# HGRN2 sample states: forget-gate multiply on GpSimd during the first four attention levels, instead of on VectorE in the loop behind them

## The chip, the cores and the metric

The kernel runs on one core of a Trainium2 chip, with its five engines: TensorE (PE in the rows, PEld for its weight loads), VectorE (DVE), ScalarE (ACT), GpSimd (POOL) and SyncE (SP). The metric is the device time of one launch in microseconds, lower is better.

## The reference, cut to what matters

The program is one inference step of a two-layer decoder trunk, for 256 prompt positions and 8 sample rows of one token each. Each layer has three mixer branches (RWKV-7, HGRN2, spatial gating), a merge, and a PEER expert block. The change is in HGRN2. Its state update per sample row, one token long, is this line with a single position:

```python
b = jnp.cumsum(l_c, axis=1)                       # l_c = log of the forget gate
...
b_last = b[:, -1]
s = (jnp.exp(b_last)[..., None] * s
     + jnp.einsum("bshk,bshv->bhkv", k_c * jnp.exp(b_last[:, None] - b), v_c))
```

For a sample row this is S = f * S + k v^T, with four heads of a 128 by 128 state, float32 throughout. The product f * S is the forget-gate multiply that the change moves. For the prompt the same recurrence is computed in chunks of 128 positions; its attention matrix, with a decay between every pair of positions, is built in seven "levels" of block halving.

## The kernel before

The kernel is written engine by engine, in a fixed order, with semaphores between the engines; nothing is scheduled by a planner. `S["name"]` is a semaphore. On VectorE, `done(ins, name, n)` lets the instruction raise the semaphore and then waits for it, `step(ins)` does the same with a semaphore of its own, and a bare `tt(...)` (tensor_tensor, printed as L1291) goes on without a wait.

**The levels.** For each of seven levels VectorE runs two subtractions of cumulated log gates (`lev_in`), ScalarE takes their exponential (`lev_exp`), VectorE multiplies by keys and by queries (two instructions, `lev_x`), and TensorE forms the product, 16 matmul records into banks 0 and 1 (`att_mm`), with a piece of a gate projection behind it. VectorE masks each bank into T5 or VS (`att_evac`), and GpSimd adds that to AT_ (L1818, `at_add`), two additions of 128x512 per level. T5 and VS are reused by the next level, so the masking of level n waits for the addition of level n-1. In VectorE's order a level therefore reads: mask, mask, multiply, multiply, subtract, subtract, where the subtractions belong to the level behind. The names M1, M2 are used below for the two multiplications, S1, S2 for the two subtractions, A0, A1 for GpSimd's two additions.

**The sample states.** `shs(b)` is the state of sample row b, 128 x 512 floats. ScalarE's queue loads the eight from HBM (L1101, L1102, semaphore `shs_in`) ahead of the levels. EB holds the exponentials of the cumulated log gates; for the sample columns that is the forget gate itself (`eb_done`). Behind the levels, and behind the two chunks of the prompt's output, TensorE broadcasts the value row of sample b over 128 partitions into bank 4 or 5 (an 8x512 matmul, two records, `vb_mm`), the broadcast of b waiting for `vb_evac` of b-2. VectorE then runs three instructions per b: shs = shs * f (not waited for), T5 = bank * k, shs = shs + T5. When all eight are done TensorE multiplies the states by the queries, 64 matmul records with one moving column (`hso_mm`), and from there the work goes on to a norm, to the spatial gating and to the branch merge.

GpSimd runs besides this the low halves of split weights (L1810) early in the layer and of the experts' weights (L1822) late in it.

Of the kernel before, what the change touches and what calls it, by code (L numbers as in the profile page):

```python
# [21 lines left out]
ALU = mybir.AluOpType  # L22
# [3 lines left out]
P = 128  # L26
D_MODEL = 1024
KD = D_MODEL // P
SEQ, DEC, DEPTH = 256, 8, 2
# [77 lines left out]
def build(nc, d):  # L107
    ctx = ExitStack()
    with ctx:
# [47 lines left out]
        def at(off, *dims):  # L157
            n = 1
            for x in dims:
                n *= x  # L160
            assert off + n <= ARENA, (off, n)
            v = arena[:, off:off + n]
            if len(dims) == 2:
                v = v.rearrange("p (a b) -> p a b", a=dims[0])
            if len(dims) == 3:
                v = v.rearrange("p (a b c) -> p a b c", a=dims[0], b=dims[1])
            return v
# [57 lines left out]
        HV = {n: at(o + i * NW * T, NW, T) for i, n in enumerate(names)}  # L225
# [8 lines left out]
        def shs(b):  # L234
            return SHA[:, b] if b < 5 else SHB[:, b - 5]
# [35 lines left out]
        def tka(*dims):  # L271
# [23 lines left out]

        names = """par_in smalls_in lb_in lb_exp mix_sq mix_ss mix_std h_ready shift_out z_mm z_evac xv_mm
            xv_evac zs_ready lora_in lora_mm lora_evac decay_in decay_out kk_sq kk_ss kk_std prep_done bon_done
            bon_mm mat_mm mat_evac l_mm l_evac p_mm p_evac ml_ready xt_mm xt_add x_mm x_add late_gates w_hi w_low w_plow x_done tok_mm tok_evac y_mm y_evac u_mm
            u_evac o_evac s_mm s_evac sq_mm sq_evac rq_in sr_in sr_done sr_out so_out so_in ot_mm gn_m gn_sq gn_v
            gn_std yr_done hg_in hg_sig f_ready f_ln b_ready eb_done lev_in lev_exp lev_x att_mm att_evac kh_in  # L300
            kh_exp kh_done ht_mm ht_evac ho_evac hs_mm hs_evac shs_in vs_mm vs_evac vb_mm vb_evac hso_mm hso_evac
# [5 lines left out]
        S = {n: ctx.enter_context(nc.semaphore(n)) for n in dict.fromkeys(names)}  # L307
# [23 lines left out]
        def over(ap, n):  # L331

            return ap.rearrange("p (a b) -> p a b", b=1).broadcast_to([ap.shape[0], ap.shape[1], n])
# [15 lines left out]
        def ring_pair(p):  # L349

            return p % RINGP if p < 37 else (p - 37) % RINGP
# [921 lines left out]
        def _(dve):  # L1273
# [5 lines left out]
            def step(ins):  # L1279

                steps[0] += 1
                ins.then_inc(S["dve_step"], 1)
                dve.wait_ge(S["dve_step"], steps[0])

            def done(ins, name, n):

                ins.then_inc(S[name], 1)
                dve.wait_ge(S[name], n)

            def tt(out, a, b, op):  # L1290
                return dve.tensor_tensor(out, a, b, op)  # L1291
# [40 lines left out]
            for l in range(DEPTH):  # L1332
# [174 lines left out]
                FF, U1, U2, BC, EB, KH, QH = (HV[n] for n in ("FF", "U1", "U2", "BC", "EB", "KH", "QH"))  # L1507
# [49 lines left out]
                for lev in range(1, LEV_H + 1):  # L1557
                    hx = HV[f"HX{lev % 2}"]
                    b = 1 << (lev - 1)
# [21 lines left out]
                dve.wait_ge(S["at_add"], 2 * LEV_H * (l + 1))  # L1581
                for b in range(DEC):
                    dve.wait_ge(S["vb_mm"], l * DEC + b + 1)
                    tt(shs(b), shs(b), over(EB[:, :, SEQ + b], P), ALU.mult)
                    step(tt(T5, bank[4 + b % 2][:, :].rearrange("p (a b) -> p a b", a=NW),
                            over(HG[:, 4:8, SEQ + b], P), ALU.mult))
                    done(tt(shs(b), shs(b), T5, ALU.add), "vb_evac", l * DEC + b + 1)
# [214 lines left out]
        @block.gpsimd  # L1802
        def _(pool):

            for l in range(DEPTH):

                for c in range(RT, 25):
                    pool.wait_ge(S["w_hi"], l * NSPLIT + c + 1)
                    at_tile = 2 * ring_pair(c // 2) + c % 2
                    pool.tensor_tensor(ring_r[:, at_tile], ring[:, at_tile], WZ[c % 3].bitcast(F32), ALU.subtract)\  # L1810
                        .then_inc(S["w_plow"], 1)

                for lev in range(1, LEV_H + 1):
                    for c in range(NHC):
                        pool.wait_ge(S["att_evac"], l * 2 * (LEV_H + 1) + 2 * lev + c + 1)
                        if lev > 1:
                            pool.wait_ge(S["at_add"], l * 2 * LEV_H + 2 * (lev - 2) + c + 1)
                        pool.tensor_tensor(AT_[:, c], AT_[:, c], (T5, VS)[c], ALU.add).then_inc(S["at_add"], 1)  # L1818

                def low(u, b, slot, turn):  # L1820
                    pool.wait_ge(S["hi_done"], turn + (l * NU + u + 1))
                    pool.tensor_tensor(WHL[:, b, 1], raw[:, slot], WHL[:, b, 0].bitcast(F32), ALU.subtract)\  # L1822
                        .then_inc(S["plo_done"], 1)

                with pool.Fori(0, GU // SLOTS) as i:
                    for b in range(SLOTS):
                        low(b, b % 2, b, i * SLOTS)
                with pool.Fori(0, NODD // 2) as i:
                    for b in (1, 3):
                        low(GU + b, 1, b, i * SLOTS)  # L1830
# [97 lines left out]
```

## Time and profile before

| what | value |
|---|---|
| runs shown | 3088.27, 3092.19, 3093.40 us |
| their median | 3092.19 us |
| the profiled execution's own time | 3089.66 us |
| its span, first to last instruction | 3087.8 us |
| busy share PE / DVE / ACT / POOL | 92% / 61% / 37% / 20% |
| mean granted TensorE clock | 0.952 |

The busy shares are averages over the whole span. The change concerns two short stretches in each of the two layers: the levels, from about 378 to 416 us, and the loop over the sample states, from about 435 to 453 us, with the same again about 1529 us later. A row of a timeline has its start, the duration in us, the engine, the line, the operation, out<-in with shapes, a count of instructions run together as one row, and in brackets the idle time ahead of it and what ended that. The granted clock is TensorE's, as a share of 2.4 GHz; 0.50 is 1.2 GHz.

### The profile page before, as it was taken

The page shows a single profiled execution, that of the slowest core. Times are in us where ns is not written, and L with a number is a line of the kernel's source. Part 1 is how long each engine was busy: PE and PEld are TensorE (multiplying, and loading weights), DVE is VectorE, ACT ScalarE, POOL GpSimd, SP SyncE. Part 2 cuts the span into 40 slices and gives each one's busy share as a digit, 9 for nine tenths or more (in the row PEclk, how much of TensorE's full clock was granted, in tenths as well). Part 3 has the DMA queues.
Part 4 walks back from the last instruction along what each step waited for, and adds up shares of the span by engine and source line. Part 5 has one row for each costly group of instructions (what it writes and reads, how often), then busy time and mean ns, then how long its engine had stood idle before and what let it go on. Part 6 is the DMA issues. An engine that isn't in the chain of part 4 may idle for free.

```text
span 3087.8 us, 55843 instructions
## 1 busy us (share of the span) xinstructions
PE 2842.2 (92%) x21498; PEld 2659.4 (86%) x21498; DVE 1878.0 (61%) x2841; ACT 1145.9 (37%) x1822; POOL 602.9 (20%) x242
## 2 busy tenths in 40 slices
PE   7699778899999999999987996798999999999998
PEld 6688557799899999999986885577999999999997
DVE  4854664259856666666658537443696666666665
ACT  3312211045543335555443112101455433455553
POOL 0400020018842220000021001100388322200000
PEclk9899887999999999999998998789999999999998
DMA  5222212335543335555551222114355433455553
GB/s 198 82 85 69 88 42 82 123 117 163 159 141 122 122 121 172 182 178 179 160 201 45 95 69 86 58 55 150 123 160 161 135 119 120 129 177 181 179 179 120
DMA packets 114369, 396.02 MB, mean 128 GB/s; under 512 B 18194, under 2 KB 19730, under 8 KB 112852
## 3 DMA queue, kind: packets, MB, share of 16 engines
q1 hardware_dynamic: 105444, 381.28, 37.9%
q10 hardware_dynamic: 8816, 13.27, 1.4%
q8 instruction: 70, 1.15, 0.1%
q14 instruction: 39, 0.32, 0.0%
HBM read 385.44 MB, written 8.53 MB: 128 GB/s over the span
## 4 chain that ended last, share of the span: by engine, by line
PE 61%; issue 22%; POOL 10%; DVE 6%; ACT 1%; DMA 0%; POOLq 0%; ACTq 0%; SPq 0%; DVEq 0%
PE bank L450 61%; POOL WHL L1822 8%; DVE arena L1291 4%; POOL ring_r L1810 1%; ACT arena L954 1%; POOL arena L1818 1%; DVE arena L1516 0%; DVE arena L1400 0%; DVE arena L1295 0%; DVE hT L1299 0%; DVE arena L1299 0%; DVE NRM L1309 0%; DVE arena L1532 0%; DMA COM<-com 0%; DVE arena L1365 0%
## 5 line engine op out<-in xcount | busy, mean ns | idle before, releaser
L450 PE MATMUL bank<-HHL,WHL 128*128 128x264 f32 x6144 | 795.6, 287 | 27.2 <-POOL WHL L1822 21.5
L450 PEld LDWEIGHTS bank<-HHL,WHL 128*128 128x128 f32 x6144 | 763.7, 190 | 37.5 <-POOL WHL L1822 28.6
L450 PE MATMUL bank<-AHL,WHL 128*128 128x264 f32 x6144 | 748.7, 284 | 0.0
L450 PEld LDWEIGHTS bank<-AHL,WHL 128*128 128x128 f32 x6144 | 748.5, 188 | 0.0
L1822 POOL TENSOR_TENSOR WHL<-raw,WHL 128x1024 fp32r<-128x1024 f32 x188 | 484.8, 2586 | 997.6 <-ACT WHL L954 997.6
L954 ACT ACTIVATE WHL<-raw 128x1024 fp32r<-128x1024 f32 x512 | 542.3, 1060 | 336.1 <-PE bank L450 334.4
L1291 DVE TENSOR_TENSOR WHL<-raw,WHL 128x1024 fp32r<-128x1024 f32 x324 | 394.8, 1218 | 26.2 <-ACT WHL L954 26.2
L450 PEld LDWEIGHTS bank<-arena 64*64 64x64 f32 (+3 forms) x3200 | 274.8, 165 | 136.7 <-DVE arena L1291 99.4
L450 PE MATMUL bank<-arena 64*64 64x64 f32 (+7 forms) x3200 | 301.3, 256 | 96.2 <-DVE arena L1291 91.2
L954 ACT ACTIVATE arena<-bank 128x264 f32<-128x264 f32 (+6 forms) x248 | 110.5, 463 | 728.8 <-PE bank L450 636.7
L1291 DVE TENSOR_TENSOR AHL<-ACTS,AHL 128x528 fp32r<-128x528 f32 x256 | 181.3, 708 | 277.9 <-ACT AHL L954 277.9
L954 ACT ACTIVATE ACTS<-bank 128x264 f32 (+32 forms) x438 | 147.9, 338 | 489.8 <-PE bank L450 489.5
L450 PE MATMUL bank<-hT,ring 128*128 128x264 f32 (+1 forms) x1280 | 315.7, 399 | 14.2 <-DVE hT L1299 11.7
L1291 DVE TENSOR_TENSOR arena<-arena 128x512 f32<-128x512 f32 (+9 forms) x254 | 263.1, 1055 | 105.5 <-ACT arena L954 59.5
L450 PEld LDWEIGHTS bank<-hT,ring 128*128 128x128 f32 x1280 | 242.4, 194 | 62.3 <-DVE hT L1299 12.5
L450 PE MATMUL bank<-OHG,OHE 128*128 128x128 bf16 x1584 | 209.0, 297 | 0.0
L1291 DVE TENSOR_TENSOR ACTS<-ACTS,bank 128x240 f32<-128x240 f32 (+21 forms) x132 | 71.2, 539 | 184.0 <-ACT ACTS L954 183.8
L450 PEld LDWEIGHTS bank<-OHG,OHE 128*128 128x128 bf16 x1584 | 168.7, 118 | 8.0
L954 ACT ACTIVATE AHL<-ACTS 128x528 fp32r (+1 forms) x256 | 160.9, 628 | 2.1 <-PE bank L450 2.1
L450 PE MATMUL bank<-arena,ring 128*128 128x264 f32 x640 | 151.2, 397 | 7.8 <-DVE arena L1291 4.4
L1291 DVE TENSOR_TENSOR arena<-bank,arena 128x264 f32<-128x264 f32 (+2 forms) x132 | 74.7, 578 | 128.2 <-PE bank L450 127.5
L450 PEld LDWEIGHTS bank<-arena,ring 128*128 128x128 f32 x640 | 125.3, 196 | 31.2 <-DVE arena L1291 4.6
(128 smaller groups left out, 2104.9 us busy)
## 6 DMA issues: line engine op xcount, KB each, us to landing
raw<-down SPq DMA_DIRECT2D x256, 512.0 KB, 3.5
raw<-up SPq DMA_DIRECT2D x256, 512.0 KB, 3.5
ring<-wm SPq DMA_DIRECT2D x100, 1024.0 KB, 5.0
arena<-hs ACTq DMA_DIRECT2D x2, 1280.0 KB, 5.8
o_hs<-arena ACTq DMA_DIRECT2D x2, 1280.0 KB, 4.5
arena<-cm SPq DMA_DIRECT2D x2, 1160.0 KB
arena<-rs SPq DMA_DIRECT2D x4, 512.0 KB, 6.2
o_rs<-arena ACTq DMA_DIRECT2D x4, 512.0 KB, 5.6
```

What stands on the lines that cost most here:

```text
L450: return pe.matmul(out, lhsT, rhs, start=start, stop=stop)
L954: return act.activation(out, in_, fn, **kw)
L1291: return dve.tensor_tensor(out, a, b, op)
L1810: pool.tensor_tensor(ring_r[:, at_tile], ring[:, at_tile], WZ[c % 3].bitcast(F32), ALU.subtract)\
L1818: pool.tensor_tensor(AT_[:, c], AT_[:, c], (T5, VS)[c], ALU.add).then_inc(S["at_add"], 1)
L1822: pool.tensor_tensor(WHL[:, b, 1], raw[:, slot], WHL[:, b, 0].bitcast(F32), ALU.subtract)\
```

## The change

VectorE's loop loses the multiply by the forget gate, and waits for the new semaphore `shs_f` in its place. GpSimd gets the eight multiplies, two behind its two additions in each of levels 1 to 4. Ahead of the first it waits for the loaded states and for EB. Nothing else is changed; no transfer is added or moved.

```diff
@@ VectorE, the loop behind the levels
                 for b in range(DEC):
                     dve.wait_ge(S["vb_mm"], l * DEC + b + 1)
-                    tt(shs(b), shs(b), over(EB[:, :, SEQ + b], P), ALU.mult)
+                    dve.wait_ge(S["shs_f"], l * DEC + b + 1)
                     step(tt(T5, bank[4 + b % 2][:, :].rearrange("p (a b) -> p a b", a=NW),
                             over(HG[:, 4:8, SEQ + b], P), ALU.mult))
                     done(tt(shs(b), shs(b), T5, ALU.add), "vb_evac", l * DEC + b + 1)
@@ GpSimd, at the end of each level's two additions
                         pool.tensor_tensor(AT_[:, c], AT_[:, c], (T5, VS)[c], ALU.add).then_inc(S["at_add"], 1)
+                    if lev <= 4:
+                        if lev == 1:
+                            pool.wait_ge(S["shs_in"], 32 * (l + 1))
+                            pool.wait_ge(S["eb_done"], l + 1)
+                        for b in (2 * lev - 2, 2 * lev - 1):
+                            pool.tensor_tensor(shs(b), shs(b), over(HV["EB"][:, :, SEQ + b], P), ALU.mult)\
+                                .then_inc(S["shs_f"], 1)
```

On GpSimd, in the levels of the first layer, a single run of 14 additions stands before:

```order
15 L1818 TENSOR_TENSOR arena<-arena 128x512 x14
16 L1825 UNCONDITIONAL_BRANCH
```

and after the change:

```order
15 L1818 TENSOR_TENSOR arena<-arena 128x512 x2
16 L1824 TENSOR_TENSOR arena<-arena 128x512 x2
17 L1818 TENSOR_TENSOR arena<-arena 128x512 x2
18 L1824 TENSOR_TENSOR arena<-arena 128x512 x2
19 L1818 TENSOR_TENSOR arena<-arena 128x512 x2
20 L1824 TENSOR_TENSOR arena<-arena 128x512 x2
21 L1818 TENSOR_TENSOR arena<-arena 128x512 x2
22 L1824 TENSOR_TENSOR arena<-arena 128x512 x2
23 L1818 TENSOR_TENSOR arena<-arena 128x512 x6
24 L1832 UNCONDITIONAL_BRANCH
```

The additions (L1818) of levels 1 to 4 now each have two gate multiplies (L1824) behind them; those of levels 5 to 7 stand in one run as before.

On VectorE, in the loop over the sample states of the first layer, the difference between the two kernels is this (arena<-arena is the gate multiply and the addition, arena<-bank,arena the product with k):

```order
 L1291 TENSOR_TENSOR arena<-arena,bank 128x512
-L1291 TENSOR_TENSOR arena<-arena 128x512
 L1291 TENSOR_TENSOR arena<-bank,arena 128x512
-L1291 TENSOR_TENSOR arena<-arena 128x512 x2
+L1291 TENSOR_TENSOR arena<-arena 128x512
 L1291 TENSOR_TENSOR arena<-bank,arena 128x512
-L1291 TENSOR_TENSOR arena<-arena 128x512 x2
+L1291 TENSOR_TENSOR arena<-arena 128x512
```

One of three instructions is gone for each state; the product with k is now the first one behind TensorE's broadcast.

## Rows read from the trace of the kernel before

**Rows 1.** Timeline of VectorE in the levels: start, us, engine, line, operation

```profile
378.26 2.50 DVE L1291 TENSOR_TENSOR arena<-arena 128x512 f32<-128x512 f32 x4
380.95 0.69 DVE L1291 TENSOR_TENSOR arena<-bank,arena 128x512 f32<-128x512 f32 x1 [0.19 <-PE bank L450]
...
382.63 3.77 DVE L1291 TENSOR_TENSOR arena<-arena 128x512 f32<-128x512 f32 x4
...
387.41 0.69 DVE L1291 TENSOR_TENSOR arena<-bank,arena 128x512 f32<-128x512 f32 x1 [0.26 <-PE bank L450]
388.13 3.79 DVE L1291 TENSOR_TENSOR arena<-arena 128x512 f32<-128x512 f32 x4
```

**Rows 2.** Timelines of VectorE and GpSimd in one level, in short windows

```profile
381.72 1.27 POOL L1818 TENSOR_TENSOR arena<-arena 128x512 f32<-128x512 f32 x1 [263.90 <-DVE arena L1291]
...
382.95 1.71 POOL L1818 TENSOR_TENSOR arena<-arena 128x512 f32<-128x512 f32 x1
...
382.63 0.90 DVE L1291 TENSOR_TENSOR arena<-arena 128x512 f32<-128x512 f32 x1
...
383.46 1.75 DVE L1291 TENSOR_TENSOR arena<-arena 128x512 f32<-128x512 f32 x1
```

**Rows 3.** Timeline of GpSimd and VectorE early in the first layer

```profile
111.03 1.26 DVE L1291 TENSOR_TENSOR arena<-V,arena 128x1056 f32<-128x1056 f32 x1
...
112.32 3.30 DVE L1291 TENSOR_TENSOR arena<-arena 128x1056 f32<-128x1056 f32 x1
...
112.16 2.34 POOL L1810 TENSOR_TENSOR ring_r<-ring,WZB 128x1024 fp32r<-128x1024 f32 x1 [8.18 <-ACT WZB L954]
```

**Rows 4.** Timeline of GpSimd in the levels, one level of the steady ones

```profile
387.23 2.94 POOL L1818 TENSOR_TENSOR arena<-arena 128x512 f32<-128x512 f32 x2 [2.57 <-DVE arena L1291]
```

**Rows 5.** Timeline of TensorE in the levels: a middle level and the last

```profile
385.26 2.05 PE L450 MATMUL bank<-arena 128*128 128x128 f32 x16 [1.68 <-DVE arena L1291]
...
412.81 3.58 PE L450 MATMUL bank<-arena 128*128 128x128 f32 x16 [3.46 <-DVE arena L1291]
```

**Rows 6.** Line 1102, the later of the two loads of the states

```profile
L1102 ACTq DMA_DIRECT2D arena<-hs x2: 450/450/450, 363.5 to 1892.7; - x2
...
DMA to landing us min/median/max: 7.2/7.3/7.4
```

**Rows 7.** Timeline of VectorE in the loop over the sample states

```profile
436.37 0.69 DVE L1291 TENSOR_TENSOR arena<-arena 128x512 f32<-128x512 f32 x1 [3.23 <-PE bank L450]
436.98 0.68 DVE L1291 TENSOR_TENSOR arena<-bank,arena 128x512 f32<-128x512 f32 x1
437.69 1.42 DVE L1291 TENSOR_TENSOR arena<-arena 128x512 f32<-128x512 f32 x2
...
442.67 0.69 DVE L1291 TENSOR_TENSOR arena<-arena 128x512 f32<-128x512 f32 x1 [0.18 <-PE bank L450]
...
452.49 0.69 DVE L1291 TENSOR_TENSOR arena<-arena 128x512 f32<-128x512 f32 x1
```

**Rows 8.** Timeline of TensorE in and behind that loop, and in layer two's

```profile
435.11 1.98 PE L450 MATMUL bank<-arena,CP 8*128 8x512 f32 x4
438.44 1.12 PE L450 MATMUL bank<-arena,CP 8*128 8x512 f32 x2 [1.35 <-DVE arena L1291]
...
440.49 2.07 PE L450 MATMUL bank<-arena,CP 8*128 8x512 f32 x2 [0.94 <-DVE arena L1291]
...
453.24 13.81 PE L450 MATMUL bank<-arena 128*128 128x1 f32 x64 [2.18 <-DVE arena L1291]
...
1969.72 10.57 PE L450 MATMUL bank<-arena,CP 8*128 8x512 f32 x10 [0.94 <-DVE arena L1291]
```

**Rows 9.** Windows: length, busy us of PE, PEld, DVE, ACT, POOL, then PEclk

```profile
436.00:440.00 4.00, 2.21 (x5) 0.48 (x3) 3.53 (x6) 0.00 (x0) 0.00 (x0) 1.00 0.92 326
...
442.00:453.00 11.00, 8.80 (x9) 1.99 (x8) 10.22 (x16) 0.00 (x0) 0.00 (x0) 0.50 0.00 0
453.00:467.00 14.00, 13.77 (x65) 13.77 (x65) 0.18 (x1) 0.00 (x0) 0.00 (x0) 0.50 0.00 0
```

More of the change, by code:

```diff
@@ L297, in build @@
             xv_evac zs_ready lora_in lora_mm lora_evac decay_in decay_out kk_sq kk_ss kk_std prep_done bon_done
-            bon_mm mat_mm mat_evac l_mm l_evac p_mm p_evac ml_ready xt_mm xt_add x_mm x_add late_gates w_hi w_low w_plow x_done tok_mm tok_evac y_mm y_evac u_mm
+            bon_mm mat_mm mat_evac l_mm l_evac p_mm p_evac ml_ready xt_mm xt_add x_mm x_add late_gates w_hi w_low w_plow shs_f x_done tok_mm tok_evac y_mm y_evac u_mm
             u_evac o_evac s_mm s_evac sq_mm sq_evac rq_in sr_in sr_done sr_out so_out so_in ot_mm gn_m gn_sq gn_v
```

## The prediction

> **What bounds the kernel now.** The page gives TensorE 92% of the span, but the change touches two stretches in which it waits. So I read the timelines of each engine there, first the levels, then the loop behind them, then how long VectorE's and GpSimd's instructions are when both run, and last the granted clock.
>
> In the levels VectorE sets the pace. From the mask at 380.95 us to the same mask one level on is 5.51 us, of which VectorE waits 0.26 us, for TensorE [rows 1]. TensorE is idle 1.68 us ahead of each level's matmuls, until VectorE's multiplications are done [rows 5], and GpSimd is idle 2.57 us of each 5.51 [rows 4]. A microsecond put on VectorE here is a microsecond of the kernel, up to that 0.26; a microsecond put on GpSimd alone is free.
>
> In the loop the pace is shared. VectorE's chain for one state is multiply, product, addition: products start at 436.98 and the next multiply ends with the row that begins 437.69, so a state takes 2.05 to 2.12 us. TensorE's broadcast of a state takes 1.12 us at 438.44, but 2.07 us at 440.49 [rows 8], since the granted clock falls from 1.00 to 0.50, from 2.4 to 1.2 GHz [rows 9]. At 442.67 VectorE waits for it [rows 7]. From there on the two engines need about the same time for a state, so VectorE's third instruction is nearly covered by TensorE.
>
> **What the change removes: the loop.** The removed multiply occupies VectorE for 0.61 us (436.98 less 436.37) [rows 7], eight times per layer. If VectorE alone counted, the gain would be 8 x 0.61 = 4.9 us, and with its short waits for TensorE about 5.3. I walk it instead, with 0.72 us from product to addition (437.69 less 436.98, start to start), so 1.44 us per state on VectorE, and about 0.05 us from addition to broadcast. Product 0 starts when the multiply did, at 436.37; additions 0 and 1 end at about 437.8 and 439.2. Broadcasts 0 and 1 are over at 437.09 [rows 8]. Broadcast 2 runs from 437.85 to 438.95, broadcast 3 from 439.3 to 440.4, both still at 1.12 us. Additions 2 and 3 end at 440.7 and 442.1. With the clock down from about 440.4 as before, broadcast 4 runs from 440.7 to 442.8 at 2.07 us, and 5, 6 and 7 follow back to back, since VectorE needs only 1.44: 444.8, 446.9, 449.0. Product and addition 7 end at 450.5. Before, the last addition ended at 453.2 (452.49 plus 0.69) [rows 7]. The gain is **2.7 us per layer**. Bounds: 1.4 us if the clock is down from broadcast 2 on (six broadcasts of 2.07 from 437.85 end at 450.3, plus 1.5 is 451.8), and 5.3 us if it stays up to the end (eight times 1.44 from 436.37 is 447.9). I take 2.7 because the stretch that is slow now, 442 to 453 us, had TensorE busy 8.80 of 11 us and 453 to 467 us had it busy 13.77 of 14, and the clock did not rise in either [rows 9]: broadcasts in closer order will not hold it up.
>
> **What it adds: GpSimd's own time.** An addition of the same size takes 1.27 us when it is not disturbed [rows 2], so two gates are 2.54 us against 2.57 us of idle time [rows 4]. Were that all, it would just fit. GpSimd's lag matters little in any case: an addition has to be done only by the masking of the next level, 5.5 us later. The wait for the loaded states costs nothing: issued at 363.5 and landed after 7.3 us [rows 6], they are there 10 us before the first gate. Nothing stands behind GpSimd's waits but the additions themselves.
>
> **What it adds: time on VectorE.** This is the term that decides. Ahead of the first addition VectorE runs M1, M2, S1, S2 in 2.50 us; in every later level, with GpSimd's additions beside them, the same four take 3.77 to 3.79 us [rows 1]. The short windows show how [rows 2]: A0 runs its 1.27 us beside a mask, which reads PSUM and one SBUF operand, and neither is stretched (0.69 us). M1, with two SBUF operands, is stretched to 0.90 until A0 is over. A1 is then recorded from 382.95 for 1.71 us instead of 1.27, waiting for M1, and M2, recorded from 383.46, takes 1.75 instead of 0.61: **1.14 us lost to one addition of GpSimd**. So an instruction of GpSimd and one of VectorE with two SBUF operands run one after the other. The same early in the layer: a 1056-element instruction of 1.26 us takes 3.30 beside a GpSimd instruction of 2.34 [rows 3], 2.04 us lost.
>
> Now the gates. A1 ends at 384.66, and M2 runs behind it to 385.21. The first gate has been waiting since A1's end, as A1 had waited for M1, so it goes next, ahead of S1; then S1; then, by the same turn, the second gate ahead of S2. Both gates fall into VectorE's row of four two-operand instructions, and each costs it 1.14 us. What is late next: S2 is followed by the mask of the next level, for which TensorE's product (1 us for each bank) has long been ready, so the 0.26 us wait for the second bank vanishes; but A0 then starts while M1 is nearly due, and takes that back from M1. I credit nothing. Levels 1 to 4 thus take 2.28 us more each, 8 x 1.14 = **9.1 us per layer**. Bounds for a gate that blocks: 1.14 and the full 1.27 us of the record, 9.1 to 10.2 us per layer. ScalarE's exponential and TensorE's matmuls stay hidden, since the delay is inside VectorE's own chain.
>
> The Trainium skill has a rule that speaks against this change. Its page "SBUF — State Buffer", section "SBUF: two separate sides", says that VectorE with two SBUF inputs and GpSimd reading SBUF share a port pair as an exclusive lock: whichever starts first has it for the whole instruction and the other fully blocks. The trace agrees in kind and nearly in size, 1.14 us lost to a 1.27 us instruction [rows 2]. By the rule taken strictly the price would be 20.3 us in both layers, by the rows it is 18.2.
>
> **A small term: TensorE's clock in the levels.** TensorE's idle time ahead of each level's matmuls grows from 1.68 to about 4.0 us. Ahead of the last level it is 3.46 us now, and the matmuls behind it take 3.58 instead of 2.05 us [rows 5]. So some levels may run at the low clock. In levels 2 to 5 it is covered, since VectorE needs 3.8 us from M2 to the next mask; in the others it could cost a microsecond. I put it at nothing, with 0 to 1 us per layer as bounds.
>
> **The sum.** Layer two repeats the pattern: the same row of ten records, 10.57 us with the same 0.94 us idle ahead, at 1969.72 [rows 8]. Per layer 9.1 - 2.7 = 6.4 us slower; both layers 12.8. Against the profiled execution's 3089.66 us that is 3102.5. It lies 2.5 us under the median of the runs shown, 3092.19, so I predict 3092.2 + 12.8 = **3105.0 us**, 0.4% slower. Its own bounds: 2 x (9.1 - 5.3) = 7.6 at the least, 2 x (10.2 - 1.4 + 1) = 19.6 at the most, so 3099.8 to 3111.8.
>
> **The rivals.**
>
> *One gate of each pair slips past S2.* If VectorE keeps its turn once, the second gate runs beside the two masks of the next level (2 x 0.69 us), which lose nothing beside GpSimd, and only one gate per level is paid: 4 x 1.14 = 4.6 us per layer. 2 x (4.6 - 2.7) = 3.8, 3096.0 us. Against it: A1 got in between M1 and M2 in every level, and back-to-back instructions of GpSimd leave no gap. Chance 0.16.
>
> *The gates are longer than the additions.* Their gate operand repeats one value over 128 elements, and no row of GpSimd shows such an operand. Where GpSimd needs, say, twice the time, every gate blocks 1.27 us longer: 16 x 1.27 = 20.3 more, 3125.3 us. Then GpSimd needs 8.0 us a level and lags too. For it there is only the missing row; against it, VectorE's multiply of the same form took 0.61 to 0.69 like its plain ones. Chance 0.10, with half of it below 3114.
>
> *Faster or no change: the gates don't block VectorE.* If the contention hung on the pair of plain operands and the gates' repeated operand spared it, GpSimd's idle 2.57 us would take the gates for nothing, and the loop's gain would stand alone: 2 x 2.7 = 5.4 us, 3086.8 us, and to 3081.6 with the high clock to the end of the loop. It decides at less than 0.34 us lost per gate (2.7 / 8). Against it stand the two places in which both engines met, each with nearly the whole of GpSimd's instruction lost. Chance 0.10.
>
> *The clock stays up through the loop and behind it.* Denser broadcasts would keep 2.4 GHz, the loop would give 5.3 us, and the 64 matmuls behind it, 13.81 us at 0.50 [rows 8, 9], at best half: 2 x (9.1 - 5.3 - 6.9) = -6.2, 3086.0 us. Against it: these same shapes kept TensorE busy 13.77 of 14 us without lifting the clock. Chance 0.04.
>
> **How the numbers follow.** Forecast 0.60, one gate slipping 0.16, longer gates 0.10, no blocking 0.10, clock held 0.04. A measurement of this kernel can tell about 0.2%, 6.2 us, from no change. Faster by more: half of the no-blocking case and half of the held clock, 0.07. Within it: one gate slipping, and the other halves, less some of the slipping case that ends above 3098.4, 0.20. Slower: 0.73. The range takes in the forecast with its bounds, the slipping case and half of the longer gates: 3095 to 3114 us.
>
> **What would show it.** In the profile after: VectorE's rows of four in levels 2 to 5 at about 6.1 us instead of 3.79, and 3.8 in level 6; a level at 7.8 us against 5.51; GpSimd's gates with records of 1.3 to 1.8 us; the loop from 17 to about 14 us, with broadcasts back to back at 2.07 us and the clock at 0.50 from its middle. Rows of four at 4.9 us would be the slipping gate, at 3.8 no blocking, and above 7 longer gates. The prediction is wrong if VectorE's instructions in the levels are not stretched, or if the clock holds in the loop.

## The result and the profile after

The changed kernel takes 3097.37 us (median of 10 runs, 3095.69 to 3100.99), the kernel before 3092.41 us (median of 10, 3088.02 to 3093.74). The ratio is 1.002, with a 95% interval of 1.0011 to 1.003: the change makes the kernel slower, by 3.4 to 9.3 us. The prediction was 3105.0 us in a range from 3095 to 3114: the direction was right and the time lies in the range, but the forecast slowdown of 12.8 us is more than twice the 5.0 us between the two medians. In that it was wrong.

The timeline of VectorE in the levels and in the loop, of the kernel after, answers to [rows 1, 7]:

```profile
387.32 5.47 DVE L1291 TENSOR_TENSOR arena<-arena 128x512 f32<-128x512 f32 x4
392.72 1.40 DVE L1291 TENSOR_TENSOR arena<-bank,arena 128x512 f32<-128x512 f32 x2
394.16 5.71 DVE L1291 TENSOR_TENSOR arena<-arena 128x512 f32<-128x512 f32 x4
...
400.71 0.69 DVE L1291 TENSOR_TENSOR arena<-bank,arena 128x512 f32<-128x512 f32 x1 [0.25 <-DVE arena L1291]
...
415.52 3.88 DVE L1291 TENSOR_TENSOR arena<-arena 128x512 f32<-128x512 f32 x4
...
448.06 0.69 DVE L1291 TENSOR_TENSOR arena<-bank,arena 128x512 f32<-128x512 f32 x1 [3.33 <-PE bank L450]
...
454.60 0.69 DVE L1291 TENSOR_TENSOR arena<-bank,arena 128x512 f32<-128x512 f32 x1 [0.77 <-PE bank L450]
...
460.67 0.69 DVE L1291 TENSOR_TENSOR arena<-arena 128x512 f32<-128x512 f32 x1
```

The row of four (M1, M2, S1, S2) has grown from 3.77 us to between 5.47 and 5.71 us in levels 2 to 5, and is back at 3.88 in level 6, where no gate runs. Behind two of the four rows the two masks follow without a wait between them (1.40 us in one row); behind the two others the second mask waits 0.25 and 0.17 us. In the loop VectorE waits for TensorE from the fifth product on.

GpSimd's timeline, to hold against [rows 4]:

```profile
386.40 2.94 POOL L1818 TENSOR_TENSOR arena<-arena 128x512 f32<-128x512 f32 x2 [261.36 <-DVE arena L1291]
389.30 2.95 POOL L1824 TENSOR_TENSOR arena<-arena 128x512 f32<-128x512 f32 x2
393.48 2.93 POOL L1818 TENSOR_TENSOR arena<-arena 128x512 f32<-128x512 f32 x2 [1.23 <-DVE arena L1291]
...
414.70 2.94 POOL L1818 TENSOR_TENSOR arena<-arena 128x512 f32<-128x512 f32 x2 [1.23 <-DVE arena L1291]
```

From the additions at 386.40 to those at 414.70 are 28.30 us for four levels, 7.07 each, where it was 5.51. GpSimd is still idle 1.23 us in each level: it isn't the bound, VectorE is. And TensorE's timeline, to hold against [rows 8]:

```profile
446.70 1.98 PE L450 MATMUL bank<-arena,CP 8*128 8x512 f32 x4
449.53 1.12 PE L450 MATMUL bank<-arena,CP 8*128 8x512 f32 x2 [0.85 <-DVE arena L1291]
450.98 1.25 PE L450 MATMUL bank<-arena,CP 8*128 8x512 f32 x2 [0.33 <-DVE arena L1291]
452.43 7.42 PE L450 MATMUL bank<-arena,CP 8*128 8x512 f32 x8 [0.20 <-DVE arena L1291]
461.41 13.81 PE L450 MATMUL bank<-arena 128*128 128x1 f32 x64 [1.56 <-DVE arena L1291]
```

The granted clock (last figure but two of a window's row) falls in the loop as before:

```profile
450.00:452.00 2.00, 1.67 (x4) 0.29 (x2) 1.90 (x4) 0.00 (x0) 0.00 (x0) 0.96 0.81 328
452.00:454.00 2.00, 1.80 (x3) 0.61 (x3) 1.76 (x3) 0.00 (x0) 0.00 (x0) 0.50 0.00 0
```

The yardstick for what follows is the stretch from GpSimd's first addition of the levels to the first of the 64 matmuls behind the loop, in each layer. It holds all that the change touches, and nothing of the differences from one execution to the next that lie elsewhere.

| kernel | layer one, us | layer two, us | against before, both layers |
|---|---|---|---|
| before | 381.72 to 453.24: 71.52 | 1910.92 to 1982.47: 71.55 | |
| after | 386.40 to 461.41: 75.01 | 1918.96 to 1993.98: 75.02 | +6.96 |

The profiled execution of after has a span of 3099.2 us, 11.4 more than before. 6.96 of that is in these stretches; 4.68 was there before the levels of layer one began (386.40 against 381.72), in work that the change doesn't touch: the first kernel of the experiments below has the same code up to there and begins its levels at 382.51. Between and behind the stretches the two agree within 0.2 us. Most runs of after lie near 3095.7 or near 3100.5, and most of before near 3089 or near 3093, a spread of the same size; so 6.96 us is the better figure for the change, as far as one trace of each kernel gives it, and it lies in the interval.

Layer one taken apart: four levels +6.27, the last levels -0.48, the transposes and output matmuls up to the loop +1.1, the broadcast's start +0.1, the loop up to the 64 matmuls 16.87 to 13.35 us, which is -3.52. The -0.48 and +1.1 come from where the low clock falls: TensorE's matmuls there are the same in number, and the 16 of the transposes take 3.64 us where they took 2.40.

### The profile page after: what moved, and what is told of

The parts are those of the page before. It is cut to its first block, busy times and chain, and to the rows that moved or that the text cites. A ratio compares the mean times of both kernels' runs of the same rounds, so it can differ in the third digit from the quotient of the medians.

```text
span 3099.2 us, 55845 instructions
## 1 busy us (share of the span) xinstructions
PE 2855.2 (92%) x21498; PEld 2673.2 (86%) x21498; DVE 1881.0 (61%) x2825; ACT 1146.4 (37%) x1822; POOL 625.6 (20%) x258
## 4 chain that ended last, share of the span: by engine, by line
PE 61%; issue 21%; POOL 10%; DVE 6%; ACT 1%; DMA 0%; POOLq 0%; ACTq 0%; SPq 0%; DVEq 0%
PE bank L450 61%; POOL WHL L1829 8%; DVE arena L1291 4%; POOL ring_r L1810 1%; POOL arena L1824 1%; ACT arena L954 1%; POOL arena L1818 1%; DVE arena L1516 0%; DVE arena L1400 0%; DVE arena L1295 0%; DVE hT L1299 0%; DVE arena L1299 0%; DVE NRM L1309 0%; DMA COM<-com 0%; DVE arena L1532 0%
## 5 line engine op out<-in xcount | busy, mean ns | idle before, releaser
L450 PEld LDWEIGHTS bank<-arena 64*64 64x64 f32 (+3 forms) x3200 | 285.0, 170 | 146.1 <-DVE arena L1291 106.9
L450 PE MATMUL bank<-arena 64*64 64x64 f32 (+7 forms) x3200 | 313.9, 262 | 103.7 <-DVE arena L1291 98.7
L450 PEld LDWEIGHTS bank<-hT,ring 128*128 128x128 f32 x1280 | 242.8, 194 | 62.1 <-DVE hT L1299 12.5
L1818 POOL TENSOR_TENSOR arena<-arena 128x512 f32<-128x512 f32 x28 | 42.4, 1531 | 543.6 <-DVE arena L1291 543.6
```

The lines of the kernel that those rows point to most:

```text
L450: return pe.matmul(out, lhsT, rhs, start=start, stop=stop)
```

## The experiments

**Does a gate block VectorE less because its operand is one value repeated?** The short windows of the kernel after show that one gate stretches a subtraction to 1.53 us, and not to 1.75 as an addition does to M2 [rows 2]. Each short window cuts out one instruction, of the kernel after:

```profile
389.30 1.50 POOL L1824 TENSOR_TENSOR arena<-arena 128x512 f32<-128x512 f32 x1
...
389.81 1.53 DVE L1291 TENSOR_TENSOR arena<-arena 128x512 f32<-128x512 f32 x1
...
390.76 1.49 POOL L1824 TENSOR_TENSOR arena<-arena 128x512 f32<-128x512 f32 x1
...
391.26 1.53 DVE L1291 TENSOR_TENSOR arena<-arena 128x512 f32<-128x512 f32 x1
```

M2 ends at 388.14 + 1.75 = 389.89; from there to the gate's end at 390.80 are 0.91 us. For an addition the same reckoning gave 1.13 us (M1's end 383.53 to 384.66). Either the gate is the shorter one, or VectorE's subtraction, which reads a repeated operand too, suffers less. To measure by, the same two subtractions in the kernel before, with no work of GpSimd beside them, and the mask behind them:

```profile
390.64 0.68 DVE L1291 TENSOR_TENSOR arena<-arena 128x512 f32<-128x512 f32 x1
...
391.24 0.68 DVE L1291 TENSOR_TENSOR arena<-arena 128x512 f32<-128x512 f32 x1
391.96 0.69 DVE L1291 TENSOR_TENSOR arena<-bank,arena 128x512 f32<-128x512 f32 x1
```

The run gives GpSimd's multiply a plain operand and leaves VectorE as it is:

```diff
-                            pool.tensor_tensor(shs(b), shs(b), over(HV["EB"][:, :, SEQ + b], P), ALU.mult)\
+                            pool.tensor_tensor(shs(b), shs(b), CP[:, 0:512].rearrange("p (a b) -> p a b", a=NW), ALU.mult)\
```

> The changed kernel, but GpSimd's gate multiplies read a plain 128x512 tile (the constants) as second operand instead of one value repeated 128 times; this changes the sample states of HGRN2, the work is otherwise the same. In the changed kernel a gate stands 1.46 us behind the other and VectorE's subtraction beside it takes 1.53 us, where an addition of GpSimd stretched a multiplication to 1.75. Theory A, the repeated operand makes the gate itself shorter in SBUF: with a plain operand the subtractions take about 1.75 us, the row of four goes from 5.5 to about 5.95 us, a level from 7.07 to about 7.5, and the kernel gets 2 x 4 x 0.45 = 3.6 us slower than the changed one (+9 to +10 us against the kernel before). Rival B, it is VectorE's subtraction, which itself reads a repeated operand, that suffers less: nothing changes, 1.53 us, level 7.07 us, +5 to +6 us against the kernel before.

Measured: 3102.18 us (median of 6), ratio to before 1.0033 (1.0021 to 1.0045). The two engines' timelines in the levels, GpSimd's and then VectorE's, and the short windows on one gate and the subtractions:

```profile
385.41 3.39 POOL L1824 TENSOR_TENSOR arena<-arena,CP 128x512 f32<-128x512 f32 x2
390.03 2.93 POOL L1818 TENSOR_TENSOR arena<-arena 128x512 f32<-128x512 f32 x2 [1.23 <-DVE arena L1291]
...
412.57 2.94 POOL L1818 TENSOR_TENSOR arena<-arena 128x512 f32<-128x512 f32 x2 [1.23 <-DVE arena L1291]
...
383.43 5.92 DVE L1291 TENSOR_TENSOR arena<-arena 128x512 f32<-128x512 f32 x4
...
387.09 1.71 POOL L1824 TENSOR_TENSOR arena<-arena,CP 128x512 f32<-128x512 f32 x1
...
387.60 1.75 DVE L1291 TENSOR_TENSOR arena<-arena 128x512 f32<-128x512 f32 x1
...
393.43 1.75 DVE L1291 TENSOR_TENSOR arena<-arena 128x512 f32<-128x512 f32 x1
395.11 1.75 DVE L1291 TENSOR_TENSOR arena<-arena 128x512 f32<-128x512 f32 x1
396.78 0.68 DVE L1291 TENSOR_TENSOR arena<-bank,arena 128x512 f32<-128x512 f32 x1
```

The subtraction is stretched to 1.75 us and the gate's record is 1.71, both exactly as with an addition; a level takes 7.51 us (22.54 for three from 390.03), 0.44 more than in the changed kernel. Theory A holds, B falls: what a GpSimd instruction takes from VectorE hangs on GpSimd's own operands. That a multiply has the same figures as an addition shows too that the operation makes no difference. The time came out 10.2 us above before by the ratio, where 9 to 10 were expected: the levels bring the 3.5 us over the changed kernel, and the rest is TensorE's clock, which falls earlier in this kernel's loops (13.83 and 13.82 us, against 13.35).

**Do the two terms add?** First the levels' price alone: VectorE's multiply is back in the loop, and GpSimd's stay.

```diff
                     dve.wait_ge(S["shs_f"], l * DEC + b + 1)
+                    tt(shs(b), shs(b), over(EB[:, :, SEQ + b], P), ALU.mult)
```

> The changed kernel with VectorE's multiply put back into the loop as well, so that the states are multiplied by the gate twice; this gives the price of GpSimd's eight multiplies in the levels alone. If the two terms add: the levels cost 4 x 1.57 = 6.3 us per layer, the loop has its old length of 16.8 us, and the kernel is 12.5 us slower than the one before (ratio 1.004). Rival, the two terms depend on each other through the clock: the sum differs from 12.5 by 2 us or more.

Then the loop's gain alone: from the kernel before, the multiply goes, and nothing takes its place.

```diff
-                    tt(shs(b), shs(b), over(EB[:, :, SEQ + b], P), ALU.mult)
```

> The kernel before with the gate multiply left out altogether, on both engines; the sample states are then not decayed. This gives the gain of the loop alone. By the trace of the changed kernel the loop and what stands ahead of the 64 matmuls behind it is 3.4 us shorter per layer, so 6.8 us faster than before (ratio 0.998); by my prediction's walk it was 2.7 and 5.4 us. The loop runs at 1.7 to 1.9 us a state once the clock is at 0.50, and the clock falls there as before. Rival: without the delay from the levels the clock falls at another moment and the gain is 1.4 or 5.3 us per layer.

Measured: the levels alone 3104.79 us (median of 5), ratio 1.0041 (1.0027 to 1.0055), which is 12.7 us slower; the loop alone 3084.19 us (median of 9), ratio 0.9976 (0.9966 to 0.9986), 7.4 us faster. TensorE's timeline of the loop, first of the levels-only kernel, then of the loop-only kernel:

```profile
451.15 10.54 PE L450 MATMUL bank<-arena,CP 8*128 8x512 f32 x10 [0.94 <-DVE arena L1291]
463.86 13.81 PE L450 MATMUL bank<-arena 128*128 128x1 f32 x64 [2.17 <-DVE arena L1291]
```

```profile
440.78 7.43 PE L450 MATMUL bank<-arena,CP 8*128 8x512 f32 x8 [0.33 <-DVE arena L1291]
449.79 13.81 PE L450 MATMUL bank<-arena 128*128 128x1 f32 x64 [1.58 <-DVE arena L1291]
```

The stretches are 78.50 and 78.48 us in the levels-only kernel, +13.91 in all, and 68.03 and 68.06 in the loop-only kernel, -6.98. The sum is +6.93, and the changed kernel has +6.96. The terms add to 0.03 us. In the levels-only kernel four levels take 28.30 us, +6.27 as in the changed kernel. The small clock terms (-0.48 and +1.1 per layer) are in the levels-only kernel too and not in the loop-only one, so they cancel out of the comparison. Where I expected 12.5 us for the levels alone, the stretches say 13.9; my rival's mark of 2 us is not reached.

Whether the longer levels cause these clock terms is only half shown. From the additions of level 5 to the first broadcast TensorE has the same work in every kernel here, and the traces have, in us:

| kernel | layer one | layer two |
|---|---|---|
| before, and the loop alone | 31.36, 31.35 | 31.38, 31.38 |
| after, and the levels alone | 32.00, 32.01 | 32.01, 32.00 |
| plain operands | 32.04 | 31.93 |
| gates on GpSimd behind level 7, and gates in VectorE's gap (both below) | 32.01, 32.01 | 31.42, 31.38 |
| the two kernels with four banks (below) | 30.04, 30.04 | 31.37, 31.35 |

In layer two the 0.6 us go with the longer levels in every trace. In layer one kernels with the old levels have all three values, so there the difference can't be put down to the change.

**Is it the place?** If the price is the meeting with VectorE's two-operand instructions, the same gates on the same engine should cost nothing where VectorE waits. In the next run GpSimd does all eight behind the additions of level 7.

```diff
-                    if lev <= 4:
-                        if lev == 1:
-                            pool.wait_ge(S["shs_in"], 32 * (l + 1))
-                            pool.wait_ge(S["eb_done"], l + 1)
-                        for b in (2 * lev - 2, 2 * lev - 1):
-                            pool.tensor_tensor(shs(b), shs(b), over(HV["EB"][:, :, SEQ + b], P), ALU.mult)\
-                                .then_inc(S["shs_f"], 1)
+                pool.wait_ge(S["shs_in"], 32 * (l + 1))
+                pool.wait_ge(S["eb_done"], l + 1)
+                for b in range(DEC):
+                    pool.tensor_tensor(shs(b), shs(b), over(HV["EB"][:, :, SEQ + b], P), ALU.mult)\
+                        .then_inc(S["shs_f"], 1)
```

> The eight gate multiplies on GpSimd, but all behind the additions of level 7, where VectorE waits for TensorE most of the time. Theory: the price in the levels was the meeting with VectorE's two-operand instructions, so here it vanishes; 8 gates of about 1.25 us start at about 419.6 us on the time scale of the kernel before and end at about 430, the loop starts at 436. Levels at 5.51 us as before, the loop as short as in the changed kernel: 2 x 3.4 = 6.8 us faster than before. Rival: the gates meet the two updates of SH (0.7 us each, a multiplication and an addition) and TensorE waits for these: up to 1 us back per layer, 4.8 us faster than before.

Measured: 3085.61 us (median of 11), ratio 0.9982 (0.9973 to 0.9991), 2.8 to 8.3 us faster than before. GpSimd's timeline behind the levels, with two of its eight gates in short windows, and VectorE's beside it:

```profile
420.87 8.54 POOL L1822 TENSOR_TENSOR arena<-arena 128x512 f32<-128x512 f32 x8
...
421.87 1.04 POOL L1822 TENSOR_TENSOR arena<-arena 128x512 f32<-128x512 f32 x1
...
427.91 1.49 POOL L1822 TENSOR_TENSOR arena<-arena 128x512 f32<-128x512 f32 x1
...
427.80 0.69 DVE L1291 TENSOR_TENSOR arena<-arena 128x512 f32<-128x512 f32 x1 [7.37 <-PE bank L450]
```

The first seven gates have records of 1.04 us and begin 1.00 us apart, where an undisturbed addition has 1.27. That answers the question above a second time: a gate with a repeated operand is 0.23 us shorter than an addition by itself. VectorE idles 7.37 us beside them, and only its update of SH, from 427.80, meets the very end of the seventh gate and the eighth, from 427.91. Here VectorE was ahead of the eighth: its record stays at 0.69 us, and it is the gate that grows, to 1.49. The levels are back at 5.51 us (388.89, 394.40, 399.91 for the additions). The stretches are 68.75 and 68.17 us, -6.15 in both layers; most of the 0.8 us that are missing to the loop alone is layer one's clock, in the table above. The theory's 6.8 us and the rival's 4.8 both lie in the interval, so the time alone doesn't part them; the timeline does, since the update of SH at 427.80 is 0.69 us long and waits for TensorE. The place is what made the changed kernel slow.

**Is GpSimd needed at all?** The same gap of VectorE takes the eight multiplies on VectorE itself. In the kernel before it looks like this, the update of SH behind 6.40 us of waiting:

```profile
425.49 0.69 DVE L1291 TENSOR_TENSOR arena<-arena 128x512 f32<-128x512 f32 x1 [6.40 <-PE bank L450]
```

```diff
                 done(dve.memset(SH, 0.0), "hs_evac", 3 * l + 1)
+                dve.wait_ge(S["shs_in"], 32 * (l + 1))
+                for b in range(DEC):
+                    ins = tt(shs(b), shs(b), over(EB[:, :, SEQ + b], P), ALU.mult)
+                step(ins)
...
-                    tt(shs(b), shs(b), over(EB[:, :, SEQ + b], P), ALU.mult)
```

> The kernel before, with the eight gate multiplies still on VectorE, but ahead of the two updates of SH, where it waits 6.4 us for TensorE. GpSimd gets nothing. Theory: the place decides, not the engine. Eight multiplies of 0.61 us are 4.9 us and fit into the 6.4 us, so levels and updates stay as they are and the loop is as short as with the multiply left out: 3.5 us per layer, 7 us faster than before (ratio 0.9977), as the run with the multiply left out. Rival: the first update of SH comes late and TensorE waits for it; then 1 to 2 us per layer come back and it is 3 to 5 us faster.

Measured: 3083.65 us (median of 8), ratio 0.9974 (0.9964 to 0.9985). VectorE's timeline behind the levels:

```profile
420.27 5.20 DVE L1291 TENSOR_TENSOR arena<-arena 128x512 f32<-128x512 f32 x8
427.61 0.69 DVE L1291 TENSOR_TENSOR arena<-arena 128x512 f32<-128x512 f32 x1 [2.14 <-PE bank L450]
```

The eight take 5.20 us and VectorE still waits 2.14 us for TensorE behind them: nothing is late. Moved 16 us ahead, without another engine, the removal of the multiply from the loop is worth 4.6 to 11.1 us by the interval. The stretches are 68.68 and 68.05 us, -6.34 in both layers. The rival's 3 to 5 us would need TensorE to wait for the update of SH, and it is VectorE that waits. Theory and place are confirmed.

**What holds the loop, once the multiply is out?** VectorE waits for TensorE in it at the low clock. Four banks in place of two take the waiting of the broadcasts for the additions away; the first use of bank 3 waits for the last reading of the prompt's state from it.

```diff
-                    if b >= 2:
-                        pe.wait_ge(S["vb_evac"], l * DEC + b - 1)
-                    mm(bank[4 + b % 2][:, 0:W], ident[0:DEC, b:b + 1].broadcast_to([DEC, P]),
+                    if b == 3:
+                        pe.wait_ge(S["hs_evac"], 3 * l + 3)
+                    if b >= 4:
+                        pe.wait_ge(S["vb_evac"], l * DEC + b - 3)
+                    mm(bank[(4, 5, 2, 3)[b % 4]][:, 0:W], ident[0:DEC, b:b + 1].broadcast_to([DEC, P]),
```

(VectorE's product reads the same bank.) One run has this on top of the last kernel, one on the kernel before.

> The last kernel, with TensorE's broadcasts in four banks instead of two, so that a broadcast waits for the addition four states back and not two. Theory: without the multiply the loop is held by TensorE at the low clock, 1.70 to 1.94 us a state from the fourth on, where VectorE needs 1.45. With four banks more broadcasts are made before the clock falls, and the loop is VectorE's: 8 x 1.45 = 11.6 us instead of 13.3, so 3.4 us faster than with two banks in both layers, 10.4 us faster than before. Rival, the handshake is not what holds it: a broadcast at the low clock takes 1.7 us even back to back, the gain is under 1 us per layer.

> The kernel before, only with the broadcasts in four banks. My reading of the loop before was that both engines hold it, 2.05 us a state by VectorE and 2.07 by TensorE. With four banks TensorE's part goes, and VectorE's 8 x 2.05 = 16.4 us remain of 16.8: 0.4 us per layer, under 1 us in all, no change that can be measured. Rival: the loop was TensorE's before as well, and gets 1.5 us shorter or more per layer.

Measured: on top of the last kernel 3079.83 us (median of 5), ratio 0.9962 (0.9949 to 0.9976); on the kernel before 3091.96 us (median of 10), ratio 0.9998 (0.9988 to 1.0007), no change. VectorE's first and last row of the loop and TensorE's row for the broadcasts, of the first of the two:

```profile
435.99 0.69 DVE L1293 TENSOR_TENSOR arena<-bank,arena 128x512 f32<-128x512 f32 x1 [3.23 <-PE bank L450]
...
446.87 0.69 DVE L1293 TENSOR_TENSOR arena<-arena 128x512 f32<-128x512 f32 x1
...
434.74 10.67 PE L450 MATMUL bank<-arena,CP 8*128 8x512 f32 x16
```

and, of the kernel before with four banks:

```profile
436.08 0.69 DVE L1293 TENSOR_TENSOR arena<-arena 128x512 f32<-128x512 f32 x1 [3.23 <-PE bank L450]
...
451.77 0.69 DVE L1293 TENSOR_TENSOR arena<-arena 128x512 f32<-128x512 f32 x1
```

Without the multiply the loop takes 11.57 us (435.99 to 447.56), where two banks gave 13.3: VectorE's 8 x 1.45, and no wait in it. With the multiply it takes 16.38 us (436.08 to 452.46) against 16.8. So before the change the loop was VectorE's with TensorE just below it, and four banks were worth nothing; once VectorE's part is shortened TensorE is next, and they are worth 1.7 us per layer in the loops. This kernel is 7.4 to 15.8 us faster than the one before by the interval. Its median is the lowest of all that ran, 3.8 us below the last kernel's, but the two intervals overlap: the gain of the banks is shown by the loops (1.7 us in each layer), and not by the times.

## Why the prediction was right and wrong

**The mechanism was right.** GpSimd's and VectorE's two-operand instructions run one after the other, both gates of a level fall into VectorE's row of four, and VectorE's chain sets the levels' pace. The levels-only and the late run show it from both sides. The rivals in which the gates don't block, or in which one slips past S2, are out: a row of four would have stayed at 3.8 us, or come to 4.9, and it is 5.47 to 5.71. That the gates might be longer than the additions is out as well: they are shorter.

**The step that failed is the size of a gate's price.** The prediction took 1.14 us, the stretch of M2 beside an addition [rows 2], for each of eight gates, 9.1 us per layer. Measured are 6.27. The difference of 2.85 us has two parts. The first is the operand. I had noted that no row shows a repeated operand on GpSimd, but the rivals let it make the gates longer or harmless, and not a fifth shorter, which they are. The run with plain operands costs 2.00 us a level and the changed kernel 1.57, so the operand is 0.44 x 4 = 1.8 us per layer. The second is how the 1.14 us were read. They are a record of 1.75 us less 0.61 us from one start to the next; but records overlap, so like was not compared with like. From start to start S1 takes 0.60 us in the kernel before and 1.68 with a plain gate beside it, S2 0.72 (the mask behind it follows a little later by itself) and 1.67. That is 1.08 and 0.95 us, 2.03 a level and not 2.28, and 0.25 x 4 = 1.0 us per layer. The credit that was set to nothing was rightly set: in that run the second mask no longer waits (-0.24 us), and M1 takes it back (0.84 us from start to start before, 1.05 in that run). My lower bound for a blocking gate, 1.14 us, was a single value called a bound; what a gate cost was 0.78 on average.

**The loop's term was too small.** 2.7 us was forecast, 3.52 measured. The walk was right up to the fifth broadcast, which began where it said, 4.37 us behind the first product (452.43 less 448.06; the walk has 4.33). From there it took 2.07 us for each broadcast, and the four run in 7.42 us, 1.86 each. The row of 2.07 us [rows 8] is again a record and not a pace. Two matmul records of the kernel after, at the low clock, in short windows:

```profile
453.45 1.06 PE L450 MATMUL bank<-arena,CP 8*128 8x512 f32 x1
...
454.30 1.06 PE L450 MATMUL bank<-arena,CP 8*128 8x512 f32 x1
```

Each lasts 1.06 us by its record, and the next begins 0.85 us after it: 0.21 us of a record lies under the next one. Four times 0.21 is the 0.8 us that is missing.

**The clock.** It fell in the middle of the loop, as the trace of before bore out and the held-clock rival denied. In the levels TensorE drops to the low clock in every other level, as its timeline of the kernel after shows:

```profile
397.01 3.61 PE L450 MATMUL bank<-arena 128*128 128x128 f32 x16 [3.24 <-DVE arena L1291]
...
404.09 2.05 PE L450 MATMUL bank<-arena 128*128 128x128 f32 x16 [1.62 <-DVE arena L1291]
...
411.17 3.53 PE L450 MATMUL bank<-arena 128*128 128x128 f32 x16 [3.24 <-DVE arena L1291]
```

That is hidden in the length of a level, as forecast: those of 3.61 and 2.05 us are equally long (7.07 us). It isn't quite hidden from the masks. The 3.61 us end at 400.62, and the second mask begins at 400.71 behind its 0.25 us of waiting, which the profile puts down to VectorE itself; M1 is then shorter by as much (0.93 us, where it is 1.13 behind masks that didn't wait). Behind the levels the clock does show: the stretch from the transposes to the loop is 1.1 us longer in both layers than in the trace before, and the last levels 0.5 us shorter. This was bounded by 0 to 1 us per layer, and put at nothing; 0.65 came in these traces, in layer one perhaps by chance, as the table shows.

Together, per layer: 9.1 - 2.7 = 6.4 was forecast; 6.27 + 0.7 - 3.5 = 3.5 came, the 0.7 being the clock and 0.1 us at the first broadcast. Both failures of the sum point the same way, the price too high and the gain too low, so the forecast was nearly twice what the stretches show. In a sum that is the difference of two terms, errors of three tenths in each make nearly half of the result. That the time lay in the range is luck: it is below the forecast's own bounds, 3099.8 to 3111.8, and the range held it only because it was widened to 3095 for a gate that slips past S2, which did not happen.

**The page on the SBUF lock.** The Trainium skill's "SBUF — State Buffer", section "SBUF: two separate sides", has the loser blocked for the whole instruction. The trace agrees that they exclude each other, and in both orders: in the levels VectorE's instruction is stretched, and in the run with the gates behind level 7 VectorE was first and the gate grew. But what VectorE loses is less than the GpSimd instruction takes by itself: from start to start 0.85 us beside S1 (1.45 less 0.60) and 0.74 beside S2 (1.46 less 0.72), to a gate that takes 1.00 alone. The records of 1.49 and 1.71 us can't be taken as the price at all, since they hold GpSimd's own waiting. The rule taken strictly gave 20.3 us with the 1.27 us of an addition, and would give 16 with the gate's own 1.00; the eight levels with gates grew by 12.5.

## What to carry to other kernels

Before work is moved to GpSimd "because it idles", look at what VectorE does at that moment. Beside VectorE instructions that read two SBUF operands, most of GpSimd's time is VectorE's time, and here the removed 0.61 us instruction came back as 0.78 us in a place where VectorE was the bound. The better question was when and not where: VectorE itself had a gap of 6.4 us, 16 us ahead, and the same eight instructions cost nothing in it. When a price or a pace is read from rows, take it from one start to the next: a record's length holds waiting and overlap, and both terms of this sum were mis-sized in part by it. And when an engine's part of a shared loop is cut, look at once at the handshake with the other: two more banks were worth nothing before, and 1.7 us per layer after.

## What the runs showed of the hardware

- What a GpSimd instruction takes from VectorE depends on GpSimd's operands. With two plain operands of 128x512 a VectorE instruction beside it has a record of 1.75 us in place of 0.68; with one operand a value repeated 128 times, 1.53 us. By itself such a gate has a record of 1.04 us, and the next begins after 1.00; the record of an undisturbed addition is 1.27.
- Which of the two engines was stretched went by which began first, where the starts can be told apart. VectorE's update of SH began 0.11 us ahead of a gate and kept its 0.69 us; the gate took 1.49. In layer two of the same kernel it is 0.69 and 1.53.
- VectorE instructions that read PSUM and one SBUF operand are not stretched beside GpSimd: 0.68 to 0.69 us throughout.
- TensorE's clock stays at 0.50 through work that keeps it busy nearly all the time. The window over the 64 one-column matmuls, of the kernel after:

```profile
461.00:475.00 14.00, 13.59 (x64) 13.59 (x64) 0.36 (x1) 0.00 (x0) 0.00 (x0) 0.50 0.00 0
```

With broadcasts back to back, in four banks, it doesn't hold either. Two windows of that kernel, TensorE busy throughout:

```profile
436.00:438.00 2.00, 2.00 (x6) 0.90 (x5) 1.93 (x3) 0.00 (x0) 0.00 (x0) 1.00 0.94 302
...
440.00:442.00 2.00, 2.00 (x4) 0.86 (x3) 1.90 (x4) 0.00 (x0) 0.00 (x0) 0.50 0.00 0
```

Why work of these shapes leaves the clock low was not tried, and stays open.
